# Four rows per token in memory, written plainly by the experts and summed at the end, in place of one accumulated row

## The reference

```python
logits = (xt @ w_router) + b_router                  # xt: 512 x 1024, 32 experts
top_val, top_idx = lax.top_k(logits, TOP_K)          # TOP_K = 4
gates = jax.nn.softmax(top_val, axis=-1)
...
hid = x_pad[toks] @ w1[e] + b1[e]                    # 1024 x 2048 per expert
glu = jnp.minimum(hid[..., :D_FF], SWIGLU_LIMIT)
lin = jnp.clip(hid[..., D_FF:], -SWIGLU_LIMIT, SWIGLU_LIMIT)
act = glu * jax.nn.sigmoid(SWIGLU_ALPHA * glu) * (lin + 1)
y = (act @ w2[e] + b2[e]) * wts[:, None]             # 1024 x 1024 per expert
...
h = h + y summed over the 4 experts of each token;   out = rms_norm(h, norm_final)
```

## Time and profile before

| | |
|---|---|
| median of 3 runs | 2201.04 us (2199.01 to 2213.47) |
| profiled execution | 2208.45 us |
| its span, first to last instruction | 2206.7 us |
| mean granted TensorE clock | 0.935 |
| TensorE busy | 1975.7 us, 90% of the span |
| HBM read and written | 472.71 MB and 19.96 MB |

### The profile page before, as it was taken

How to read it: one execution, slowest core, us unless ns; L and a number is a source line. 1 busy time by engine, 2 the same in 40 slices (tenths; PEclk the granted TensorE clock), 3 DMA queues, 4 the chain that set the end, 5 groups by cost and what they waited for, 6 DMA issues and landing times.

```text
span 2206.7 us, 36817 instructions
## 1 busy us (share of the span) xinstructions
PE 1975.7 (90%) x15441; PEld 900.2 (41%) x15441; DVE 444.3 (20%) x899; ACT 267.3 (12%) x531; POOL 331.8 (15%) x387
## 2 busy tenths in 40 slices
PE   7898999899999999839898889888988998899894
PEld 5454555444444444513343334333333333343342
DVE  3333433433310000222010111001110101010111
ACT  2202201122210000100010001000000000100001
POOL 3000000000000000150212121222112221212112
PEclk8989999999999999868999999999999999999997
DMA  3302111002032224327999999999999999999995
GB/s 106 94 23 76 57 35 34 12 12 56 0 109 77 77 78 180 115 100 306 360 390 342 368 360 384 349 361 379 370 365 348 386 352 363 357 393 334 370 331 168
DMA packets 163598, 495.08 MB, mean 224 GB/s; under 512 B 16048, under 2 KB 88848, under 8 KB 130656
## 3 DMA queue, kind: packets, MB, share of 16 engines
q1 hardware_dynamic: 112064, 442.83, 52.6%
q0 software_dynamic: 21600, 32.83, 6.7%
q10 hardware_dynamic: 29776, 16.91, 2.7%
HBM read 472.71 MB, written 19.96 MB: 223 GB/s over the span
## 4 chain that ended last, share of the span: by engine, by line
PE 88%; issue 6%; DVE 2%; DMA 2%; POOL 2%; ACT 1%; SPq 0%; POOLq 0%; DVEq 0%; ACTq 0%
PE PS L357 35%; PE PS L1387 32%; PE PS L1399 15%; PE PS L1243 1%; PE PS L1376 1%; PE PS L1369 1%; DMA ring<-in_w_in 1%; PE PS L1320 1%; POOL tab_dram L579 1%; PE PS L1433 0%; DVE ring L959 0%; DMA x_sb<-acc_dram 0%; ACT at_sb L707 0%; PE PS L1345 0%; POOL small L542 0%
## 5 line engine op out<-in xcount | busy, mean ns | idle before, releaser
L1387 PE MATMUL PS<-ring,mix_sb 128*32 128x512 f32 x6144 | 721.9, 614 | 94.9 <-issue 92.4
L1387 PEld LDWEIGHTS PS<-ring,mix_sb 128*32 128x32 f32 x6144 | 200.2, 112 | 577.5 <-issue 574.7
L1399 PE MATMUL PS<-ring,hm_sb 128*32 128x256 f32 x6144 | 337.4, 379 | 0.9 <-ACT hm_sb L775 0.9
L357 PE MATMUL PS<-uT_sb,ring 128*128 128x512 f32 (+1 forms) x736 | 298.0, 561 | 6.5 <-DMA ring<-in_w_in 3.5
L1399 PEld LDWEIGHTS PS<-ring,hm_sb 128*32 128x32 f32 x6144 | 199.6, 110 | 146.0 <-issue 18.5
L1136 DVE TENSOR_TENSOR hm_sb<-PS,b_sb 128x768 f32<-128x768 f32 x32 | 30.6, 957 | 1019.5 <-PE PS L1387 1019.5
L357 PEld LDWEIGHTS PS<-uT_sb,ring 128*128 128x128 f32 x736 | 140.1, 209 | 158.6 <-issue 154.7
L598 POOL DMA_INDIRECT acc_dram<-hm_sb,ints x96 | 152.0, 1583 | 47.3 <-POOL ints L617 24.0
L357 PE MATMUL PS<-ring 128*128 128x129 f32 (+4 forms) x592 | 145.7, 377 | 6.8 <-DVE ring L1009 3.5
L617 POOL COPY ints<-ints 128x3 int32 (+1 forms) x32 | 5.9, 185 | 857.4 <-ACT hm_sb L786 857.4
L357 PEld LDWEIGHTS PS<-ring 128*128 128x128 f32 (+1 forms) x592 | 83.1, 193 | 65.4 <-issue 52.0
(11 more groups left out here) (240 smaller groups left out, 1114.6 us busy)
## 6 DMA issues: line engine op xcount, KB each, us to landing
ring<-in_w SPq DMA_DIRECT2D x384, 1024.0 KB, 7.9
ring<-in_w_in SPq DMA_DIRECT2D x8, 1024.0 KB, 5.2
b_sb<-in_b SPq DMA_DIRECT2D x128, 64.0 KB, 4.8
ring<-in_w_in ACTq DMA_DIRECT2D x14, 512.0 KB, 4.0
ring<-in_w_in SPq DMA_DIRECT2D x10, 512.0 KB, 5.2
ring<-m_dram POOLq DMA_DIRECT2D x16, 256.0 KB, 4.5
ring<-in_w_out SPq DMA_DIRECT2D x1, 4096.0 KB, 13.9
ring<-in_w_m_proj ACTq DMA_DIRECT2D x7, 512.0 KB, 3.8
```

The costliest lines, as they stand in the source:

```text
L357: last = nc.tensor.matmul(out, w, r, start=n == 0, stop=n == len(pairs) - 1)
L1387: last = nc.tensor.matmul(PS[32 * j:32 * j + 32, t, :].rearrange("p (c n) -> p c n", c=2), xgT[n][:, k, 32 * t:32 * t + 32], w1_c[k][:, :, ...
L1399: last = nc.tensor.matmul(PS[32 * j:32 * j + 32, 3 + t, 0:QR], actT[:, k, 32 * t:32 * t + 32], w2_c[k // 2][:, k % 2, j * QR:(j + 1) * QR] ...
```

## The change

Each pair of token and expert choice gets a row of its own: `y_dram` has 512 x 4 rows. The table now holds 4 times the token number plus the number of the choice. From this VectorE makes two indices: `idx_y` for the row to write, and `idx_x` for the token's row to gather, by dividing by four and rounding. Empty places now hold numbers past the last row, and the indirect DMAs get a bound (`bounds_check`, `oob_is_err=False`) by which such indices are left out; the spare rows and their zeroing go. The gather buffers are zeroed once instead, by GpSimd. An expert's rows are written without an add, so the writes no longer wait for those of the expert before, but only for the same buffer's earlier ones. `acc_dram`, its first store and its semaphore go; h plus b2 stays in `xs`.

At the end SyncE loads the four rows of each token (8 DMAs of two rows per token, 1 MB each, into the weight slots), GpSimd adds the third and fourth, and VectorE adds the first, the second and that sum to `xs`. Then square, root, multiply and store follow as before. The order on VectorE is: sums of tile 0 and 1, multiply of tile 0, sums of tile 2, multiply of tile 1, and so on. The branch for overfull experts is changed in the same way.

```diff
-    pair[:, :, :, 0] = (np.arange(P)[:, None] + P * np.arange(MT)[None, :])[:, :, None]
+    pair[:, :, :, 0] = TOPK * (np.arange(P)[:, None] + P * np.arange(MT)[None, :])[:, :, None] + np.arange(TOPK)
-    spare[:, :, :, 0] = T + np.arange(32)[:, None, None] + 32 * (np.arange(NQ) % TT)[None, :, None]
+    spare[:, :, :, 0] = TOPK * T + np.arange(32)[:, None, None] + 32 * (np.arange(NQ) % TT)[None, :, None]
...
-    xt_dram = dram("xt_dram", [(T + SPARE) * 4, QR], F32)
-    acc_dram = dram("acc_dram", [(T + SPARE) * 4, QR], F32)
+    xt_dram = dram("xt_dram", [T * 4, QR], F32)
+    y_dram = dram("y_dram", [T * TOPK * 4, QR], F32)
...
+    y_rows_of = y_dram.rearrange("(t k c) n -> t k (c n)", k=TOPK, c=4)
+    y_back = [view(ring, slot(2 * m), TOPK, D) for m in range(MT)]
...
         for m in range(MT):
-            sp.dma_start(xs[:, m, :], acc_rows[m * P:(m + 1) * P, :]).then_inc(x_tile_in[m], 16)
+            for k in range(0, TOPK, 2):
+                sp.dma_start(y_back[m][:, k:k + 2, :], y_rows_of[m * P:(m + 1) * P, k:k + 2, :]).then_inc(x_tile_in[m] if k == 0 else y_tile_in[m], 16)
...
-        nc.gpsimd.memset(zeros, 0.0).then_inc(zeros_ready, 1)
-        pool.wait_ge(zeros_ready, 1)
-        for rows in (xt_rows, acc_rows):
-            pool.dma_start(rows[T:T + SPARE, :], zeros[0:SPARE, :]).then_inc(spare_zeroed, 16)
...
+        pool.wait_ge(pe_h, 2 * MT)
+        for n in range(2):
+            nc.gpsimd.memset(xg[n], 0.0).then_inc(xg_zeroed, 1)
...
                 pool.indirect_dma_start(out=xg[n][:, t, :], out_offset=None, in_=xt_dram,
-                                        in_offset=bass.IndirectOffsetOnAxis(ap=idx[:, t:t + 1], axis=0)).then_inc(xg_in[n], 16)
+                                        in_offset=bass.IndirectOffsetOnAxis(ap=idx[:, t:t + 1], axis=0),
+                                        bounds_check=T * 4 - 1, oob_is_err=False).then_inc(xg_in[n], 16)
...
-                pool.indirect_dma_start(out=acc_dram, out_offset=bass.IndirectOffsetOnAxis(ap=idx[:, t:t + 1], axis=0),
-                                        in_=y_sb[n][:, t, :], in_offset=None, compute_op=ALU.add).then_inc(y_out[n], 16)
+                pool.indirect_dma_start(out=y_dram, out_offset=bass.IndirectOffsetOnAxis(ap=idx[:, t:t + 1], axis=0),
+                                        in_=y_sb[n][:, t, :], in_offset=None,
+                                        bounds_check=T * TOPK * 4 - 1, oob_is_err=False).then_inc(y_out[n], 16)
...
             pool.wait_ge(y_ready, e + 2)
-            if again:
-                pool.wait_ge(y_out[1 - n], (e + n) * 24)
+            if stored is not None:
+                pool.wait_ge(y_out[n], stored)
...
-        for m in range(MT):
+        for m in range(MT + 1):
+            if m < MT:
+                pool.wait_ge(y_tile_in[m], 16)
+                nc.gpsimd.tensor_tensor(y_back[m][:, 2, :], y_back[m][:, 2, :], y_back[m][:, 3, :], ALU.add).then_inc(y_pair, 1)
+            if m == 0:
+                continue
+            m -= 1
...
-        for m in range(MT):
-            act.wait_ge(b2_added, m + 1)
-            act.dma_start(acc_rows[m * P:(m + 1) * P, :], xs[:, m, :]).then_inc(acc_in, 16)
...
-            act.wait_ge(x_tile_in[m], 32)
+            act.wait_ge(h_done, 3 * m + 3)
...
+        def rows_of(v, x_rows, y_rows):
+            V.tensor_scalar(y_rows, v, 4.0, ct[:, K_QTR:K_QTR + 1], ALU.mult, ALU.add).then_inc(idx_xy_ready, 1)
+            dve.wait_ge(idx_xy_ready, 1)
+            st.alone(V.tensor_scalar(v, v, 0.25, -0.375, ALU.mult, ALU.add))
+            st.alone(V.tensor_scalar(v, v, ROUND, -ROUND, ALU.add, ALU.add))
+            V.tensor_scalar(x_rows, v, 4.0, ct[:, K_QTR:K_QTR + 1], ALU.mult, ALU.add).then_inc(idx_xy_ready, 1)
+
         dve.wait_ge(tab_in, 64)
-        V.tensor_scalar(idx4, tab[:, :, :, 0], 4.0, ct[:, K_QTR:K_QTR + 1], ALU.mult, ALU.add).then_inc(idx4_ready, 1)
+        rows_of(tab[:, :, :, 0], idx_x, idx_y)
...
-        for m in range(MT):
+        def whole(m):
+
+            dve.wait_ge(b2_added, MT)
+            for k in range(3):
+                dve.wait_ge(x_tile_in[m], 32)
+                if k == 2:
+                    dve.wait_ge(y_pair, m + 1)
+                V.tensor_tensor(xs[:, m, :], xs[:, m, :], y_back[m][:, k, :], ALU.add).then_inc(h_done, 1)
+                dve.wait_ge(h_done, 3 * m + k + 1)
+
+        for m in range(MT + 1):
+            if m < MT:
+                whole(m)
+            if m == 0:
+                continue
+            m -= 1
             dve.wait_ge(rstd_ready, AT_END + m + 1)
```

More of the change, by code:

```diff
@@ L43 @@
 OVW = 24
-SPARE = CAP
 ROUND = 12582912.0
@@ L226, in build @@
     b1_bc = [view(b1_sb, n * 2 * QR, 2, QR) for n in range(2)]
-    ints = sb("ints", 192, I32)
+    ints = sb("ints", 288, I32)
     drow_i, over_i = ints[:, 0:16], ints[:, 16:16 + 2 * OVW + 1]
     drow_by = drow_i.rearrange("p (m k) -> p m k", m=MT)
-    idx4 = view(ints, 68, TT, E)
-    idx_g, idx_s = [ints[:, 164 + 3 * n:167 + 3 * n] for n in range(2)], [ints[:, 170 + 3 * n:173 + 3 * n] for n in range(2)]
-    idx_ov = ints[:, 176:179]
+    idx_x, idx_y = view(ints, 68, TT, E), view(ints, 164, TT, E)
+    idx_g, idx_s = [ints[:, 260 + 3 * n:263 + 3 * n] for n in range(2)], [ints[:, 266 + 3 * n:269 + 3 * n] for n in range(2)]
+    idx_ov = [ints[:, 272 + 3 * n:275 + 3 * n] for n in range(2)]
     tabs = sb("tabs", 2 * TT * E + 2 * TT + 2 * MT * TOPK)
@@ L255, in build @@
     expert_steps = sem("expert_steps")
+    y_tile_in = [sem(f"y_tile_in{m}") for m in range(MT)]
+    y_pair, h_done = sem("y_pair"), sem("h_done")
     out_ready, out_stored = sem("out_ready"), sem("out_stored")
@@ L585, in _ @@
         pool.wait_ge(xt_stored, 16 * MT)
-        pool.wait_ge(pe_h, 2 * MT)
-        pool.wait_ge(idx4_ready, 1)
+        pool.wait_ge(xg_zeroed, 2)
+        pool.wait_ge(idx_xy_ready, 2)
         def gather(n, idx):
```

43 lines of the change are left out of this document (23 added, 20 removed).

## The result

The changed kernel takes 2215.38 us (median of 20 runs, 2209.00 to 2226.08); the kernel before took 2208.42 in the 20 runs beside it (2199.01 to 2213.47). The ratio is 1.004, with a 95% interval of 1.0026 to 1.0054: slower by 7 us by the medians and by 9 by the ratio, well inside the 1% that was called no change. The prediction said 2222 us with a range of 2209 to 2233.

The account below looks back on a forecast made before the run. TensorE, busy 1975.7 of 2206.7 us, never waits for weights inside an expert, so lighter DMA traffic gives little. Terms -1 + 0.8 - 2.4 + 23.6 = +21 on the median 2201.04 give 2222 us, range 2209 to 2233.

Parts of the forecast that it names:

- most likely of the three: Whole kernel: chance 0.52 for within 1%, 0.44 for slower by over 1%, 0.04 for faster by over 1%.
- no lock: Tail: VectorE and GpSimd work side by side, so tail +16.4 instead of +23.6 us, 2215 us; chance 0.20.
- starts shorten by 0.5 us each: Expert loop's pass starts: fetches queue behind other packets, so less traffic gives -7 us, 2215 us; chance 0.06.
- Before the loop, +0.8: Router table to first gather: four VectorE operations in a row replace one of 0.27 us, +0.8 us.
- Up to the first load, -2.4: Tail: plain writes issue faster and land 2.6 us after the third's issue, so the load comes 2.4 us sooner.
- From the load on, +23.6: Tail: 8.4 MB come back instead of 2, and the sums become add-bound: 41.3 us against 17.7, +23.6.
- The lock: Tail sums: VectorE and GpSimd block each other in both directions, costing together 8.1 us per tile.
- The loop, -1: Expert loop: less DMA traffic shortens each of 14 pass starts by 0.1 us, -1 us; bounds nothing and 7 us.
- faster by 1%: Pass starts: would have to lose 43 us in all, 3.1 each, near 2178 us; chance 0.04.
- Dearer pair add: Tail: GpSimd's pair add up to 3.4 us, +25.4, 2226 us; chance 0.25 together with a dearer bounds test.
- The bound's test: First gather and last write: testing indices might cost 0.6 us per issue, adding 3.6 us; taken as nothing.
- The signs: Trace features listed beforehand as showing the forecast right or wrong: end loads, add lengths, last multiply, write issues, pass starts.

Follow-up runs that it names:

- vector_sums: The changed kernel with VectorE adding all four rows of a token and GpSimd none; 2215.2 us, ratio 1.0031 to the kernel before.
- late_adds: The kernel before, with each odd expert's adds waiting until mid-pass, clear of the pass's start; 2212.43 us, ratio 1.0017.
- plain_all_rows: The changed kernel without the index bound: plain writes, empty places read and written as spare rows; 2221.42 us, ratio 1.0049 to the kernel before.
- skip_only: The kernel before with only the index bound added, so empty places are left out; writes still accumulate; 2196.24 us, ratio 0.994.

## Why the prediction was right, and where it was not

- **Time.** 2215.38 us lies in the range, 7 below the forecast, and within 1% as most likely of the three. Read by its parts the prediction is right at the ends and wrong in the loop, and part of the hit is luck. The change was put at +21 us and is +7.0. Half of that miss doesn't show in 2222, since this was counted from 2201.04, the median of three runs, and the kernel before takes 2208.42 in twenty. From there the same sum gives 2229, still within the range, but 14 too high. The rivals "no lock" and "starts shorten by 0.5 us each" also named 2215 us. The first of them is excluded by the traces of after and vector_sums; the second's mechanism is the one at work.
- **Before the loop, +0.8.** Measured +0.79. Since the first turn wanders by 8 us either way from run to run, the chain's rows are the better proof: four operations take 1.08 us where one took 0.27, +0.8. Of the memsets of the gather buffers and the removed stores nothing shows, as argued.
- **Up to the first load, -2.4.** From the last copy to the load's issue it was 9.54 us before and is 6.80 now: -2.7, and within the bounds of 0 and -3. The writes' 0.98 + 0.30 us held; from the third's start to the load's issue it was 2.2 where 2.6 were taken.
- **From the load on, +23.6.** Measured 2213.5 - 2172.03 = 41.5 us against 17.7: +23.8. The last multiply started 34.1 us after the load's issue, just short of the 34.7 to 36.7; the stores behind it took 6.1 to the end where 4.6 were taken (why, the runs don't show). That these two cancel is luck; the sum is nearer than its parts. Loads landed 5.2 and 7.7 us after the issue, for 4.9 and 7.4. The pair add was 2.33 alone for 2.3.
- **The lock.** "I take it that the reverse holds": it does. VectorE's multiply showed 3.29 us behind a pair add. vector_sums gained 4.4 us at the end by giving GpSimd's adds to VectorE, where two engines that can work side by side would have lost 4 to 5. The sign as worded, VectorE's adds starting only at the pair adds' ends, was imprecise: the blocked instruction may start on record and be long.
- **The loop, -1: the mis-sized term.** Measured -15, outside its bounds of 0 and -7. Two sentences of the prediction failed. One: "A lighter load on the DMA engines therefore has nothing to give inside an expert; it could only shorten the starts of passes." That was right, but what it could give there was put at 0.1 us a pass on the ground that the accumulating writes lie in the second half of the stall. late_adds shows that their moment is not what counts. The fetch waits behind the queued weights, and by the table over ten kernels it starts sooner where less is left to move. Two: "As the stall hardly varies from pass to pass" was read from the first gap alone. The earlier trace rows had the 1.62 us gap as well, and over the 14 passes that one went from 0.54 to 1.75 us, which is what a queue looks like and a fixed cost does not. The upper bound of 7 us took only the first gap's row.
- **That rival's price.** "The starts of passes shorten" put 0.5 us on each, by a queue behind other packets. That is the mechanism; it gave 1.1 us a pass, 0.8 in the second gap, and the rest in the first gap and the slow matmuls. The chance of 0.06 was too low for something that a gap with no semaphore, next to full DMA engines, had pointed to. Still, the 3.1 us per pass that it needed for "faster by 1%" were out of the change's reach: with the weights gone altogether the starts lose 3.5 us each.
- **Dearer pair add.** It did not decide: 2.33 us alone, 3.42 and 3.07 where VectorE held it up, which is the lock's time and already in the sum. The bound's test costs 0.02 us an issue at the write and 0.05 at the gather (0.996 and 1.026 us in after; 0.980 and 0.976 in plain_all_rows, which has no test).
- **The signs.** Right: eight loads over 23 us (380 GB/s from 2172 to 2195), GpSimd's adds of 2.3 us, last multiply 40.9 us after the last copy (43 said), write issues at 1.0, first gaps still 5.2 to 5.6, no wait for gathers in the loop. Missing from that list was the second gap, the one that moved.

## What to carry to other kernels

When an engine's hardware loop shows "issue" at each pass's start while the DMA engines are full, write that engine's loop out before anything else: here it gave 60 us (ratio 0.973), and what looked like 92 us of nobody's time was instruction fetches, half of it spent behind the weights, with slow matmuls after each. Take a change apart before you judge it: the index bound alone saved 12 us, the four rows per token gave back in the loop less than half of the 21 us that they cost at the end, so bound plus accumulation plus the written-out loop (2135.87 us, 0.967) beats all. And don't split elementwise work between VectorE and GpSimd on SBUF operands: here the engine that seemed free was not, and VectorE alone finished sooner.

## What the runs showed of the hardware that was not expected

- A pass's start on TensorE costs 2.8 to 3.0 us with empty DMA engines, and 5.1 to 5.8 with 400 GB/s of weights under way. A later gap adds 0 to 2 us per pass. Both end a fixed time after a packet of instructions has come: 1.9 to 2.1 us at the first gap, 1.2 to 1.6 at the second.
- The granted clock falls with each such gap: in before it is 1.00 ahead of it and 0.50 to 0.56 from 6 to 9 us after the pass's start, that is 1.2 GHz, and in after the 96 matmuls behind a gap take 12.80 us where 96 at full clock take 10.44. As an estimate from the passes' lengths it cost 3.0 us a pass in after and 3.4 in before, over the gaps themselves (mean pass 73.89 and 75.15, less the gaps, less 65.12, which is two experts of 32.56).
- Accumulation doubles q0's packets (gathers and writes together between 1050 and 2100 us, 84 of each: 16128 accumulating in before, 8064 plain in plain_all_rows), and an accumulating write takes 1.58 us to issue where a plain one takes 1.00, and at the end 3.85 us pass from its start to the next load's issue where 2.20 do.
- Indices past the bound move next to nothing: q0 carried 22.03 MB before and 14.96 in skip_only, 0.68 of it where 2048 of 3072 places are filled. The packets stay at 16128.
